# Second block: norms tile by tile, transpositions in four banks, first heads' loads ahead of the stores, reciprocals by pairs

## The chip, the cores and the metric

One core of one Trainium2 chip runs the whole program in one launch. The metric is the device time of that core in microseconds (us), the median of the runs; smaller is better.

## The reference, cut to what matters

The input is 512 tokens of width 1024 in fp32. A first transformer block (attention, neighbourhood attention, Fourier and convolution branches, a router with 16 experts) ends in `rms_norm(x, final_norm_g)`. The second block then runs two equal layers and a last norm:

```python
def rms_norm_2(x, w):
    y = xf * lax.rsqrt(jnp.mean(xf * xf, axis=-1, keepdims=True) + NORM_EPS)
    return (y * w).astype(x.dtype)

def hybrid_layer(x, ...):
    h = rms_norm_2(x, attn_norm_w)
    proj = h @ w_in
    mixed = concatenate([retention_mixer(...), dsa_mixer(...), dilated_mixer(...)])
    x = x + mixed @ w_out
    h = rms_norm_2(x, mlp_norm_w)
    return x + jnp.square(jax.nn.relu(h @ w_up)) @ w_down
```

Retention has 4 heads, the selecting attention (dsa) 4, the dilated attention 8, each 64 wide. The selecting attention scores each query against all earlier keys with 8 index heads and keeps the 128 best; the softmax runs over those.

## The kernel before, in words

Five engine programs are written out by hand and meet at semaphores. Tokens are 4 tiles of 128 rows (`X[:, i, :]`, 1024 wide), the inner dimension is 8 slices of 128 (`k`).

**Products.** A weight unit is 512 x 512. SP loads it (`unit`, L298), ACT rounds it to the short form (`hi`, L1269, into `WH`), DVE makes the remainder (`lo`, L1798, into `WL`), and PE runs three products for each of 4 slices and 4 output banks, 48 matmuls (`unit`, L715, line L736). A `blk` is two units on the same four banks. Weights lie in two slots that alternate.

**Norms of the second block.** There are five: one at the head of each layer, one ahead of each MLP, and the last. At the first block's end the tiles of the experts' output are combined on DVE (L2447 to L2453), then `final` (L2455) norms all four, and the layer's own norm follows. ACT squares and sums a tile of 1024 columns (`squares`, L1347), DVE turns four sums at once into reciprocal roots with 11 small instructions (`stats`, L1833, `rsqrt`, L1825) and scales the four tiles (`normed`, L1840). Then PE transposes (`turn_direct`, L760): 8 slices of 4 transpositions, in two banks of PSUM, so slice k waits until slice k-2 has been read. ACT rounds each slice (`split_direct`, L1337) and DVE makes its remainder (L1869). The first unit of products starts after all 32 transpositions.

**Index scores.** 24 steps (`index`, L1162 on PE, `relu`, L1659 on ACT, `index`, L2479 on DVE) stand between the output banks of the projections. In each, DVE adds a weighted score into `IX[tt]`; from step 8 on it also does one top-8 round for query tile 1 (`top_rounds`, L2496: a maximum and a replacement, 16 rounds for 128 keys). The rounds for tiles 2 and 3 stand among the six units of dilated projections, as `TOP_2` and `TOP_3` say (L113, L114). PE does the retention heads there too (`retention`, L1199).

**Attention.** `mixed_attention` (PE L933, ACT L1481, DVE L2078) takes 12 heads in 6 pairs. Per head: ACT rounds q and k (`rounded`), DVE makes remainders (`remainders`), PE scores four query tiles, DVE adds the bias and takes the extreme (`top`), ACT takes the exponential, PE transposes, ACT copies, PE multiplies with the values (`values`, L952) and then spreads the reciprocal sums of that head over 64 rows with four products against the identity (L963). DVE multiplies both (`put`). From pair 2 on PE does the output product in between, 3 matmuls per step (`product`), and the last 8 groups of 12 after the last pair (L1026). DVE adds them into X (`add`, L2113); ACT squares tile by tile as they are ready (semaphore `x5`).

**SP's order there.** Ahead of the first pair (`after_retention`, L440) SP waits until all stores of the layer are written, the one of the last projection among them, and until the retention heads have left the buffers; then it loads the bias, q, k and v of heads 4 and 5, and the two first blocks of `w_out` into `ST[0]` and `ST[1]`, which the stores have read. DVE releases PE and ACT for the attention with `sel_done` (L2601) after the last top-8 round.

The two layers are one loop of two turns on each engine.

```python
            def turn_direct(src, nk):
                for k in range(nk):
                    if k >= 2:
                        pe.wait_ge(sems["norm_lo"], T.at("norm_lo", k - 1))
                    for i in range(NT):
                        c0 = (k % 2) * 512 + i * P
                        mm = pe.transpose(TP[:, c0:c0 + P], src(i, k), IDN[:])
                    mm.then_inc(sems["norm_tr"], 1)
```

## Time and profile before

| | |
|---|---|
| median of 3 runs | 3216.89 us (3213.39 to 3218.46) |
| profiled execution, its own time | 3215.07 us |
| its span | 3213.0 us |
| PE busy (matmul) | 2753.3 us, 86% |
| DVE busy | 1742.8 us, 54% |
| ACT busy | 1271.9 us, 40% |
| ACT's rounding of a weight unit (L1275), mean of 131 | 1.91 us |
| DVE's remainder of one (L1803), mean of 131 | 2.29 us |
| loads of `w_up` units, median from issue to landing | 5.4 us |
| mean granted clock of TensorE | 0.934 |

The second block begins about 1580 us after the span's start; its two layers take about 800 us each. PE is busy for nearly all of the MLP parts; the stretches in which it is not lie around the norms, before the attention, and within it. A share of the granted clock of 1.00 is 2.4 GHz, 0.50 is 1.2 GHz.

### The profile page before, as it was taken

How to read it: one execution, taken by the hardware profiler on the slowest of the kernel's cores; microseconds unless marked ns; L12 is line 12 of the kernel's file. 1: busy time of each engine (PE TensorE's matmuls, PEld its weight loads, DVE VectorE, ACT ScalarE, POOL GpSimd, SP SyncE). 2: the span in 40 equal slices, each digit the busy share in tenths (PEclk: the TensorE clock that was granted, in tenths of full speed). 3: DMA queues.
4: the chain of work that ended last, by engine and by line, in shares of the span. 5: the costliest groups of instructions: out<-in, count | busy, mean ns of one | idle time of the engine just before them, and what ended most of it. 6: DMA issues, size and time to landing. Idle time of an engine off the chain costs nothing. (4 is left out here: it accounts for less than half of the span.)

```text
span 3213.0 us, 34356 instructions
## 1 busy us (share of the span) xinstructions
PE 2753.3 (86%) x11967; PEld 2064.3 (64%) x11967; DVE 1742.8 (54%) x2583; ACT 1271.9 (40%) x1739; POOL 114.6 (4%) x172
## 2 busy tenths in 40 slices
PE   3879989978798399999489969899999996989998
PEld 0167566556577277777376746688877573668886
DVE  1045146667575588888635755444443665544444
ACT  1033246656522177777433245222233314532222
POOL 2011000000000100000000100000000100000000
PEclk9989999989999699999779979899997997989999
DMA  8655343245253299999622442122222234222221
GB/s 316 217 159 151 114 109 91 81 103 129 90 180 118 111 354 371 386 371 366 232 61 82 118 109 85 62 95 91 91 87 63 92 99 129 65 66 92 95 100 72
DMA packets 241592, 466.35 MB, mean 145 GB/s; under 512 B 67864, under 2 KB 90640, under 8 KB 241455
## 3 DMA queue, kind: packets, MB, share of 16 engines
q1 hardware_dynamic: 226383, 413.73, 39.2%
q0 software_dynamic: 15072, 50.87, 4.7%
q8 instruction: 77, 1.26, 0.2%
q14 instruction: 60, 0.49, 0.1%
HBM read 399.83 MB, written 64.72 MB: 145 GB/s over the span
## 5 line engine op out<-in xcount | busy, mean ns | idle before, releaser
L1803 DVE TENSOR_TENSOR WL<-W,WH 128x2048 fp32r<-128x2048 f32 x131 | 300.2, 2292 | 502.2 <-ACT WH L1275 497.0
L1275 ACT ACTIVATE WH<-W 128x2048 fp32r<-128x2048 f32 x131 | 250.4, 1912 | 649.8 <-PE BKP L736 590.1
L736 PE MATMUL BKP<-hH,WH 128*128 128x512 f32 x896 | 357.4, 399 | 15.8 <-DVE hL L2201 13.2
L736 PE MATMUL BKP<-hL,WH 128*128 128x512 f32 x896 | 352.7, 394 | 0.0
L736 PE MATMUL BKP<-hH,WL 128*128 128x512 f32 x896 | 352.7, 394 | 0.0
L736 PE MATMUL BKP<-WH,aH 128*128 128x512 f32 (+1 forms) x544 | 215.3, 396 | 22.5 <-DVE aL L2396 10.4
L736 PE MATMUL BKP<-WL,aH 128*128 128x512 f32 (+1 forms) x544 | 211.4, 389 | 0.0
L736 PE MATMUL BKP<-WH,aL 128*128 128x512 f32 (+1 forms) x544 | 211.3, 388 | 0.0
L736 PEld LDWEIGHTS BKP<-hH,WH 128*128 128x128 f32 x896 | 171.4, 191 | 57.1 <-issue 20.3
L736 PE MATMUL BKP<-WH,hH 128*128 128x512 f32 (+3 forms) x512 | 201.2, 393 | 7.2 <-ACT Z L1326 3.1
L736 PE MATMUL BKP<-WH,hL 128*128 128x512 f32 (+3 forms) x512 | 194.2, 379 | 0.0
L736 PEld LDWEIGHTS BKP<-hL,WH 128*128 128x128 f32 x896 | 170.6, 190 | 36.6
L736 PEld LDWEIGHTS BKP<-hH,WL 128*128 128x128 f32 x896 | 171.4, 191 | 35.0
L736 PE MATMUL BKP<-WL,hH 128*128 128x512 f32 (+3 forms) x512 | 193.6, 378 | 0.0
L2290 DVE TENSOR_TENSOR X<-X,BKP 128x512 f32<-128x512 f32 x128 | 86.3, 684 | 144.6 <-PE BKP L736 144.6
L736 PEld LDWEIGHTS BKP<-WH,aH 128*128 128x128 f32 x544 | 103.3, 190 | 54.2 <-DVE aL L2396 21.4
L736 PEld LDWEIGHTS BKP<-WH,hH 128*128 128x128 f32 x512 | 104.5, 204 | 39.7 <-issue 24.7
L1125 PE MATMUL BKP<-WH,hH 128*128 128x512 f32 x276 | 113.9, 413 | 11.4 <-DVE WL L2416 8.1
L2416 DVE TENSOR_TENSOR WL<-W,WH 128x2048 fp32r<-128x2048 f32 x46 | 105.3, 2289 | 24.1 <-ACT WH L1614 23.8
L2416 DVE TENSOR_TENSOR WL<-G,WH 128x2048 fp32r<-128x2048 f32 x45 | 103.0, 2289 | 27.2 <-ACT WH L1614 27.2
L736 PEld LDWEIGHTS BKP<-WH,aL 128*128 128x128 f32 x544 | 103.3, 190 | 20.9
L736 PEld LDWEIGHTS BKP<-WL,aH 128*128 128x128 f32 x544 | 103.4, 190 | 19.6
(443 smaller groups left out, 5581.1 us busy)
## 6 DMA issues: line engine op xcount, KB each, us to landing
W<-in_w_expert_gu_dram SPq DMA_DIRECT2D x46, 1024.0 KB, 8.7
G<-in_w_expert_gu_dram SPq DMA_DIRECT2D x46, 1024.0 KB, 8.9
W<-in_w_in_dram SPq DMA_DIRECT2D x42, 1024.0 KB, 5.4
W<-in_w_up_dram SPq DMA_DIRECT2D x32, 1024.0 KB, 5.4
W<-in_w_down_dram SPq DMA_DIRECT2D x32, 1024.0 KB, 5.0
W<-in_w_expert_down_dram SPq DMA_DIRECT2D x24, 1024.0 KB, 8.0
G<-in_w_expert_down_dram SPq DMA_DIRECT2D x22, 1024.0 KB, 8.0
X<-in_w_in_dram SPq DMA_DIRECT2D x16, 1024.0 KB, 8.2
```

The source lines that it names most:

```text
L736: mm = pe.matmul(BK[j][:, 0:cols], lt, rh, start=start and a == 0, stop=stop and a == len(q) - 1, skip_group_check=True)
L1125: pe.matmul(dst, ah[:, k0 + kk, :], wh[:, kk, c], start=k0 + kk == 0, stop=False, skip_group_check=True)
L1275: act.activation(WH[s][:], W[s][:], ACT.Copy).then_inc(sems["w_hi"], 1)
L1803: v.tensor_tensor(WL[s][:], W[s][:], WH[s][:].bitcast(F32), ALU.subtract).then_inc(sems["w_lo"], 1)
L2290: v.tensor_tensor(xs, xs, BK[j], ALU.add).then_inc(sems[BANKS[j]], 1)
L2416: v.tensor_tensor(ring_l(m, s0), ring_w(m, s0), ring_h(m, s0).bitcast(F32), ALU.subtract).then_inc(sems["w_lo"], 1)
```

## The change

All of it is in the second block and the end of the first.

- **Norms by tile.** ACT squares half tiles of 512 columns as soon as they are summed (`half_square`, `tile_square`). DVE makes the root of one tile with 9 small instructions (`root`) and scales that tile (`tile_norm`). At the first block's end combining, the first block's norm and the layer's norm run interleaved over the tiles, and the first weight remainder (`lo`) stands ahead of them. In the attention's tail `tile_norm(j)` stands after the two additions of tile j, `lo` ahead of the first. In a layer's last MLP chunk it stands after the addition of tile j, and in the last layer the final scaling and the output do.
- **Transpositions.** Four banks (`TB`): 16 transpositions, then the first output bank of the first unit, then the other 16, then the rest (`normed_blk`).
- **Order of the loads.** SP waits for the stores after the values of heads 4 and 5 instead of before their q and k. ACT loads the table of the exponential and rounds q and k of head 4 within the copies of the last projection (`first_head`), DVE makes the remainders before `selected(3)`; `sel_done` is gone.
- **Top-8 rounds.** 8 rounds of tile 2 move into index steps 16 to 23; the others are spread one by one.
- **Reciprocals by pairs.** DVE writes the reciprocal sums out over 64 columns per head (two copies each), and PE spreads both heads with four products of 128 rows, once a pair.
- The loop over the two layers is written out, the weight slots swap from one to the other.

```diff
-TOP_2 = [2, 2, 1, 2, 1, 2, 2, 1, 2, 1]
-TOP_3 = [1] * 12 + [2] * 2
+TOP_2 = [1] * 8
+TOP_3 = [1] * 16
...
+        TINY = F[:, 1, 16:17]
+        RDW = [AT[:, c:c + 256].rearrange("p (t s c) -> p t s c", t=2, s=2) for c in (512, 1280)]
...
+        TB = [TP[:, 0:512], TP[:, 512:1024], SC[:, 0:512], SC[:, 512:1024]]
...
             def after_retention(s):
 
-                if s == 0:
-                    for b in range(3):
-                        sp.wait_ge(sems[f"st_written{b}"], T.next(f"st_written{b}", stored(STORES_2, b)))
-                        sp.sem_inc(sems["paused"], 1)
...
                 for s in range(2):
                     values(4 + s, s)
+                for b in range(3):
+                    sp.wait_ge(sems[f"st_written{b}"], T.next(f"st_written{b}", stored(STORES_2, b)))
+                    sp.sem_inc(sems["paused"], 1)
                 for u in range(2):
                     load(WOR[u], out_unit(wo, 0, u), ["side_landed0", "side_landed1", "side_back0", "side_back1"][u])
...
-                T.loop(2, layer)
+                for l in range(2):
+                    layer(l)
...
+            def normed_blk():
+
+                def turned(k):
                     for i in range(NT):
+                        mm = pe.transpose(TB[k % 4][:, i * P:(i + 1) * P], XN[:, i, k * P:(k + 1) * P], IDN[:])
                     mm.then_inc(sems["norm_tr"], 1)
+
+                def rest(j):
+                    if j == 0:
+                        for k in range(4, NK):
+                            turned(k)
+                pe.wait_ge(sems["norm_xn"], T.next("norm_xn", NT))
+                for k in range(4):
+                    turned(k)
+                unit(h, 0, "F", UN, True, False, ready="norm_lo", each=rest)
+                unit(h, 4, "F", UN, False, True, ready="norm_lo")
...
-                    pe.wait_ge(sems["head_rd"], T.next("head_rd"))
-                    for tt in range(NT):
-                        mm = pe.matmul(RD2[rows, tt * P:(tt + 1) * P], RDS[:, s, tt:tt + 1].to_broadcast([P, HD]), IDN[:], start=True, stop=True,
-                                       skip_group_check=True)
+                    if s == 1:
+                        pe.wait_ge(sems["head_rd"], T.next("head_rd", 2))
+                        for tt in range(NT):
+                            mm = pe.matmul(RD2[:, tt * P:(tt + 1) * P], RDW[tt // 2][:, tt % 2, :, :].rearrange("p s c -> p (s c)"), IDN[:],
+                                           start=True, stop=True, skip_group_check=True)
...
-                pe.wait_ge(sems["sel_done"], T.next("sel_done"))
-                mixed_attention()
-                pe.wait_ge(sems["norm_xn"], T.next("norm_xn", NT))
-                turn_direct(cols_of(XN), NK)
...
+            def half_square(i, hf, ready):
+                act.wait_ge(sems[ready], T.next(ready))
+                cols = slice(hf * UN, (hf + 1) * UN)
+                act.activation(XN[:, i, cols], X[:, i, cols], ACT.Square, scale=1.0 / 32,
+                               accum_out=SM[:, hf, i:i + 1]).then_inc(sems["norm_ss"], 1)
...
-            squares("norm", lambda i: X[:, i, :], NT, "x3")
-            act.wait_ge(sems["norm_rd"], T.next("norm_rd"))
+            hi()
+            tile_square(0, "x3")
+            for i in range(NT):
+                if i + 1 < NT:
+                    tile_square(i + 1, "x3")
+                tile_square(i, "x4")
...
+                def first_head(j):
+                    if j == 2:
+                        act.activation(TINY, IDN[:, 0:1], ACT.Exp)
+                        mixed_rounded(0, l)
+                gemm(copies(lambda j: ST[1][:, j, :], UN, 4, "st_filled1", first_head), None, False)
+                mixed_attention(l)
+                slot[0] ^= 1
                 hi()
+                for j in range(NT):
+                    for hf in range(2):
+                        half_square(j, hf, "x5")
...
+            def root(i, name, count):
+
+                v.wait_ge(sems[name + "_ss"], T.next(name + "_ss", count))
+                m, half, y, work = SM[:, 3, i:i + 1], SM[:, 3, 8 + i:9 + i], SM[:, 2, i:i + 1], SM[:, 3, 16 + i:17 + i]
+                link(v.tensor_scalar(m, SM[:, 0, i:i + 1], SM[:, 1, i:i + 1], EPS, ALU.add, ALU.add))
+                v.tensor_scalar(half, m, -0.5, None, ALU.mult)
+                link(v.tensor_scalar(y.bitcast(I32), m.bitcast(I32), -0.5, float(0x5F3759DF), ALU.mult, ALU.add))
+                for _ in range(3):
+                    link(v.scalar_tensor_tensor(work, y, half, y, ALU.mult, ALU.mult))
+                    link(v.scalar_tensor_tensor(y, work, 1.5, y, ALU.add, ALU.mult))
+                return y
+
+            def tile_norm(i, count):
+                y = root(i, "norm", count)
+                v.tensor_scalar(XN[:, i, :], X[:, i, :], y, None, ALU.mult).then_inc(sems["norm_xn"], 1)
...
-                    v.reciprocal(RDS[:, s, :], DENS[:, s, :]).then_inc(sems["head_rd"], 1)
+                    link(v.reciprocal(RDS[:, s, :], DENS[:, s, :]))
+                    for half in range(2):
+                        ins = v.tensor_copy(RDW[half][:, :, s, :],
+                                            RDS[:, s, 2 * half:2 * half + 2].unsqueeze(2).to_broadcast([P, 2, HD]))
+                    ins.then_inc(sems["head_rd"], 1)
...
-                    v.sem_inc(sems["x5"], 1)
+                        v.sem_inc(sems["x5"], 1)
+                    if j == 0:
+                        slot[0] ^= 1
+                        lo()
+                    tile_norm(j, 2)
...
+            lo()
...
+            combined(0)
+            for i in range(NT):
+                if i + 1 < NT:
+                    combined(i + 1)
+                finished(i)
+                if i:
+                    tile_norm(i - 1, 2)
+            tile_norm(NT - 1, 2)
...
                         if n >= 8:
                             top_rounds(1, 1)
+                        if n >= 16:
+                            top_rounds(2, 1)
...
-                        top_rounds(2, TOP_2[q]) if q < 10 else top_rounds(3, TOP_3[q - 10])
-                        if q == 9:
+                        top_rounds(2, TOP_2[q]) if q < 8 else top_rounds(3, TOP_3[q - 8])
+                        if q == 7:
                             selected(2)
...
+                mixed_remainders(0, l)
                 selected(3)
-                v.sem_inc(sems["sel_done"], 1)
...
+                def last_sum(hf):
+                    def go():
+                        for j in range(NT):
+                            out(j)
+                            xs = X[:, j, hf * UN:(hf + 1) * UN]
+                            v.tensor_tensor(xs, xs, BK[j], ALU.add).then_inc(sems[BANKS[j]], 1)
+                            v.wait_ge(sems[BANKS[j]], T.at(BANKS[j]))
+                            v.sem_inc(sems["x4"], 1)
+                            if hf == 1 and l == 0:
+                                tile_norm(j, 5 if j == 0 else 1)
+                            if hf == 1 and l == 1:
+                                y = root(j, "norm", 5 if j == 0 else 1)
+                                if j == 0:
+                                    v.wait_ge(sems["gf_landed"], T.next("gf_landed", 16))
+                                v.scalar_tensor_tensor(XN[:, j, :], X[:, j, :], y, GF, ALU.mult, ALU.mult).then_inc(
+                                    sems["out_ready"], 1)
+                    return go
```

## Rows read from the trace of the kernel before

**Rows 1.** Waits of PE over the span: engine, tile, line, releaser, us, times, longest
```profile
PE TPP L766 <- DVE BIG L1843: 84.6, 4, 49.5
```

**Rows 2.** Timeline of PE, first layer's head: start us, us, instruction [idle before <-releaser]
```profile
1617.43 1.97 PE L766 MATMUL TPP<-IDN,BIG 128*128 128x128 f32 x8 [49.48 <-DVE BIG L1843]
...
1627.09 0.78 PE L736 MATMUL BKP<-hH,WH 128*128 128x512 f32 x1
...
1649.77 0.20 PE L736 MATMUL BKP<-WH,hH 128*128 128x72 f32 x1
```

**Rows 3.** Windows: us, busy of PE, PEld, DVE, ACT, POOL, granted clock, DMA share, GB/s
```profile
1617.00:1627.00 10.00, 7.44 (x31) 5.83 (x32) 4.88 (x7) 4.50 (x7) 0.00 (x0) 0.50 0.00 1
...
2044.00:2048.00 4.00, 4.00 (x12) 3.23 (x12) 2.33 (x3) 2.97 (x3) 0.00 (x0) 0.50 0.02 4
```

**Rows 4.** Timeline of DVE, end of the first block, the same columns as rows 2
```profile
1581.39 0.75 DVE L2449 TENSOR_SCALAR BIG<-BIG,GATE 128x1024 f32<-128x1024 f32 x1 [20.84 <-DMA G<-y_scratch,SLOT]
...
1586.13 0.75 DVE L2449 TENSOR_SCALAR BIG<-BIG,GATE 128x1024 f32<-128x1024 f32 x1
...
1609.84 2.29 DVE L1803 TENSOR_TENSOR WL<-W,WH 128x2048 fp32r<-128x2048 f32 x1 [0.41 <-DVE X L2459]
```

**Rows 5.** Timeline of DVE between the layers: last addition, then first and twelfth instruction after
```profile
2403.24 0.69 DVE L2290 TENSOR_TENSOR X<-X,BKP 128x512 f32<-128x512 f32 x1 [2.03 <-PE BKP L736]
...
2409.63 0.17 DVE L1836 TENSOR_SCALAR SM<-SM 128x4 f32<-128x4 f32 x1
...
2411.92 2.74 DVE L1843 TENSOR_SCALAR BIG<-X,SM 128x1024 f32<-128x1024 f32 x4
```

**Rows 6.** Timeline of the end: ACT's last square, DVE's last three scalings
```profile
3200.81 1.06 ACT L1351 ACTIVATE BIG<-X 128x1024 f32<-128x1024 f32 x1 [1.57 <-DVEq L2294]
...
3205.74 4.15 DVE L2459 SCALAR_TENSOR_TENSOR BIG<-X,SM,AT 128x1024 f32<-128x1024 f32 x3 [0.16 <-DVE BIG L2459]
```

**Rows 7.** DMA issues, window 1569 to 1573: count, KB each, median us from issue to landing
```profile
W<-in_w_in_dram SPq DMA_DIRECT2D x2, 1024.0 KB, 11.0
```

**Rows 8.** Timeline of SP: the weight loads ahead of two norms
```profile
1570.25 1.20 SPq L305 DMA_DIRECT2D W<-in_w_in_dram  x2
...
1999.45 1.08 SPq L305 DMA_DIRECT2D W<-in_w_up_dram  x2
```

**Rows 9.** Timeline of PE, first layer's second norm
```profile
2034.61 1.97 PE L766 MATMUL TPP<-IDN,BIG 128*128 128x128 f32 x8 [11.81 <-DVE BIG L1843]
```

**Rows 10.** Timeline of DVE, ACT and PE at the end of the index steps
```profile
1773.00 0.56 DVE L2500 MAX8 TOP<-G 128x8 f32<-128x384 f32 x1
...
1774.47 0.56 DVE L2500 MAX8 TOP<-G 128x8 f32<-128x384 f32 x1
...
1764.00 0.60 ACT L1666 ACTIVATE F<-SCP 128x512 f32<-128x512 f32 x1 [1.82 <-DVE G L2488]
...
1766.05 1.97 PE L756 MATMUL TPP<-IDN,AT 128*128 128x128 f32 x8 [4.09 <-ACT ST L1326]
```

**Rows 11.** Timeline of SP, PE and DVE before the first layer's attention
```profile
1865.82 0.34 SPq L312 DMA_DIRECT2D ES<-in_k_dilbias_dram  x1
...
1873.69 0.48 PE L940 MATMUL SCP<-WH 128*128 128x128 f32 x1 [16.18 <-DVE WH L2083]
...
1857.77 0.68 DVE L2500 MAX8 TOP<-G 128x8 f32<-128x512 f32 x1
```

**Rows 12.** DMA issues, windows 1866 to 1868.6 and 1873.65 to 1876.8, columns as rows 7
```profile
KS<-kT_scratch SPq DMA_DIRECT2D x2, 128.0 KB, 3.1
...
KS<-kT_scratch SPq DMA_DIRECT2D x2, 128.0 KB, 7.8
```

**Rows 13.** Timeline of ACT, first pair of heads: rounding of the third head's q
```profile
1885.15 0.62 ACT L1485 ACTIVATE WH<-QS 128x512 fp32r<-128x512 f32 x1
```

**Rows 14.** Timeline of PE in the third pair of heads
```profile
1933.72 1.04 PE L963 MATMUL BKP<-IDN,F 128*64 128x128 f32 x8
1934.69 0.50 PE L940 MATMUL BKP<-WH 128*128 128x512 f32 x1
```

More of the change, by code:

```diff
@@ L700, in _ @@
             if not only_first:
-                T.loop(2, layer)
+                for l in range(2):
+                    layer(l)
             for s in range(2 if only_first else 3):
@@ L1259, in _ @@
             if not only_first:
-                T.loop(2, layer)
+                for l in range(2):
+                    layer(l)
         @block.scalar
@@ L1533, in mixed_attention @@
                 act.sem_inc(sems["head_ptc"], 2)
-                rounded(0)
                 exponential(0)
@@ L1740, in layer, with chunk @@
                 begin2("dv")
-                gemm(copies(lambda j: ST[1][:, j, :], UN, 4, "st_filled1"), None, False)
-                act.wait_ge(sems["sel_done"], T.next("sel_done"))
-                mixed_attention()
-                squares("norm", lambda i: X[:, i, :], NT, "x5")
-                act.wait_ge(sems["side_mm"], T.next("side_mm", 4 * NT))
-                hi()
-                act.wait_ge(sems["norm_rd"], T.next("norm_rd"))
-                split_direct(NK, hH[:], lambda k: AF[:, 3, k:k + 1])
-                def chunk(c, more=True):
+                def first_head(j):
[3 more added lines that the diff above has]
+                gemm(copies(lambda j: ST[1][:, j, :], UN, 4, "st_filled1", first_head), None, False)
+                mixed_attention(l)
+                slot[0] ^= 1
+                hi()
+                for j in range(NT):
+                    for hf in range(2):
+                        half_square(j, hf, "x5")
+                T.skip("side_mm", 4 * NT)
+                split_direct(NK, hH[:], lambda k: VT[:, V_MLP + l * 8 + k:V_MLP + l * 8 + k + 1])
+                def chunk(c, last=False):
                     def relu():
@@ L1761, in chunk @@
                     skip_banks()
-                    unit(None, more)
+                    if last:
+                        for j in range(NT):
+                            half_square(j, 0, "x4")
+                    unit(None, not last or l == 0)
                     skip_banks()
+                    if last:
+                        for j in range(NT):
+                            half_square(j, 1, "x4")
                 act.sem_inc(sems["paused"], 1)
                 T.loop(FF // UN - 1, chunk)
-                chunk(FF // UN - 1, False)
+                chunk(FF // UN - 1, True)
             def begin2(name):
@@ L1780, in _ @@
                     held[s] = 16 * [k for n, b, k in STORES_2 if b == s][-1]
-                T.loop(2, layer)
-                squares("norm", lambda i: X[:, i, :], NT, "x4")
+                for l in range(2):
+                    layer(l)
         @block.vector
@@ L2155, in mixed_attention @@
                 T.skip("head_o", 2)
-                remainders(0)
                 top(0, chosen)
@@ L2446, in _, with combined @@
             slot[0] = s0
-            for i in range(NT):
+            lo()
+            def combined(i):
                 v.wait_ge(sems[f"yc_landed{i}"], 32)
@@ L2618, in chunk @@
                     for hf in range(2):
-                        unit(add_x(hf, False, None if more or hf == 0 else "x4"), more or hf == 0)
+                        unit(last_sum(hf) if last else add_x(hf, False), not last or hf == 0 or l == 0)
                         skip_banks()
@@ L2622, in layer @@
                 T.loop(FF // UN - 1, chunk)
-                chunk(FF // UN - 1, False)
-            T.loop(2, layer)
-            final("norm", lambda i: XN[:, i, :], "out_ready", GF)
+                chunk(FF // UN - 1, True)
+            for l in range(2):
+                layer(l)
 def tables():
```

130 lines of the change are left out of this document (53 added, 77 removed).

## The prediction

> **What bounds the kernel now.** I began with the list of PE's waits, since PE is busy 86% of the span and only what it waits for can be taken away. The largest entry is the one on the scaled rows of a norm: 84.6 us in four waits, the longest 49.5 [rows 1]. The longest is at the first block's end and holds the gathers of the experts' output; the others are 11.8 us each. Then the timeline of the first norm: after the wait PE transposes from 1617.43 to 1627.09, 9.66 us for 32 transpositions, because two banks go round; the 96 products after them end at 1649.77, so 0.227 us each once the clock is up [rows 2]. In the ten microseconds of transpositions the granted clock is 0.50, that is 1.2 GHz, and it can stay there for four more microseconds of products [rows 3]. Ahead of the attention PE is idle for 16.18 us [rows 11]. At the end of the index steps it is idle for 4.09 us behind ACT, and ACT behind DVE [rows 10]. These are the places that the change touches, and in the rest PE is the bound.
>
> **The norms' chains on DVE.** Today 11 small instructions make four roots in 2.29 us [rows 5], 0.21 each. The new root has 9, one of them unlinked, but three take as their scalar what the instruction before or two before wrote. I take 2.0 us; bounds 1.7 (nine at 0.19) and 2.4 (nine at the old rate and three gaps of 0.16, as before the last scaling, [rows 6]). It is paid per tile.
>
> *End of the first block.* From the first combining to the first transposition are 36.0 us [rows 2, 4]. New: combining 4 x 4.74 = 19.0 [rows 4]; eight roots 16.0; four scalings with the gain 4 x 1.44 = 5.8 (4.15 for three with the gap, [rows 6]); four plain scalings 2.7 [rows 5]: 43.5. The remainder of the weights, 2.29 us [rows 4], leaves the chain but stands ahead of it: its load is issued at 1570.25 and takes 11.0 [rows 7, 8], so it lands at 1581.3, the rounding adds 1.9, the remainder ends at 1585.5, and combining starts 4.1 later than at 1581.39. Together 4.1 + 43.5 - 36.0 = **+11.6 us**. ACT's squares lie beside it.
>
> *Between the layers.* Additions follow each other every 2.72 us (0.69 and 2.03 of idle, [rows 5]). A tile now costs addition 0.69, half square with its signals 0.9 (half of 1.06, [rows 6], and reading the sum), root 2.0, scaling 0.69: 4.3, so DVE and not PE sets the pace. ACT squares the last half tile of the unit before first, then rounds, DVE makes the remainder: the chain begins near 2398.1 instead of 2395.1 and ends at 2415.3. Today the transpositions begin at 2414.7 (2.74 after 2411.92). **+0.6 us**.
>
> *After the attention, twice.* Here the groups of products take 2.72 each too, 5.44 per tile, and a tile costs DVE 1.4 + 0.9 + 2.7 = 5.0, so it nearly keeps pace. `lo` in front costs a start: load at 1999.45 [rows 8], 5.4 to land, rounded 2007, remainder done 2009.6, first tile 2012.3; the bank for the fifth group comes free at 2013.0, where PE wanted it at 2011.8: a wait of 1.3. The last group ends at 2024.0, its tile is scaled at 2028.3, against 2034.6 [rows 9]: **-6.3 us** each, -12.6.
>
> *The end.* Four tiles of 0.69 + 0.9 + 2.0 + 1.4 = 5.1 from the first addition, 8.2 before the last at 3200.0 [rows 6]: 3212.3 against 3209.9. **+2.4 us**.
>
> **Transpositions, four times.** Today 9.66 us stand ahead of the products. New: 16 transpositions, at the low clock 0.23 each, 3.65 us; products of the first bank wait for nothing that the low clock would not cost; 16 more take 1.85 us at the high clock, 3.65 at the low one. Saved 4.2 or 2.4. The transpositions did not bring the clock up, the products did [rows 3]; so I take nearly the low one: **-3.2 us** each, -12.8; bounds -4.2 and -0.4 (2.4 less the 2.0 that four further microseconds of products at 0.50, as in [rows 3], would lose, if the pause in the products keeps the clock down).
>
> The Trainium skill (TensorE: Matmul & The Clock Gate, Part 4: PE-mode transpose) says that the full clock does not engage for transpositions, which don't count as activity. By that the 16 in the midst of the first unit speak against this change: -0.4 instead of -3.2 each, and the sum would be some 11 us higher. The row of ten microseconds of transpositions at 0.50 agrees.
>
> **Top-8 rounds.** A round of 384 columns takes 1.47 us [rows 10]. Eight go into index steps 16 to 23. DVE has no idle time to speak of there: the last rectified score on ACT starts at 1764.00 as DVE's step 21 releases it, then ACT copies the transposed rows and PE goes on [rows 10]. Ahead of step 21 stand five of the new rounds: **+7.4 us** per layer, +14.8; four or six of them would be 5.9 or 8.8. What leaves the projections after it leaves PE's time untouched, PE being the bound there.
>
> **First heads' loads.** DVE has one round instead of two after 1857.77: 1859.4; two remainders of 0.7: PE begins at 1860.9 instead of 1873.69 [rows 11], -12.8. The load of the table falls into ACT's idle time. What is late next: the stores, still complete near 1865.8 [rows 11]; behind them SP issues 2 MB of `w_out`, and only then q and k of the third head, the last at 1869.5. Issued like that they took 7.8 us, not 3.1 [rows 12]: 1877.3. ACT needs them 12.8 before 1885.15 [rows 13], at 1872.4. Less traffic lies in front than today, so I take a stall of 4.0; bounds 0 and 5. **-8.8 us** per layer, -17.6.
>
> **Reciprocals.** Of two spreadings of 0.97 (1933.72 to 1934.69, [rows 14]) one is left: 6 x 0.97 = 5.8 per layer, on a PE that is the bound from the third pair on. DVE pays a link and two small copies per head, 0.55, mostly in idle time; I give back 1.0. **-9.5 us** in both; bounds -11.6 and -4.
>
> The written-out loop I cost at nothing: no row shows a wait at its turn; bounds -1 and +2.
>
> **Sum.** +11.6 +0.6 -12.6 +2.4 -12.8 +14.8 -17.6 -9.5 = -23.1. On the profiled execution's 3215.1 us that gives 3192.0; the median of the runs lies 1.8 above that execution: **3194 us**.
>
> **Rivals.** (1) *The rounds hide.* If DVE's line through the index steps had slack, the 14.8 fall away: 3179. For it: DVE has rounds enough elsewhere. Against: every rectification in that stretch names DVE. 0.13. (2) *The third head's loads come in time*, because the early heads' traffic is gone: 8.0 less, 3186. For it: 3.1 us for the same load without `w_out` ahead. Against: `w_out` still is ahead. 0.15. (3) *The start is not won*: QS of the second head, the stores or the released banks hold PE where it was: 17.6 more, 3211. That would be a change that doesn't do what it says; nothing in the rows shows such a hold. 0.06. (4) *Slower: the first unit of each norm runs at 1.2 GHz.* Its 48 products are broken by 16 transpositions after the twelfth; if the clock then comes up only after the unit, 38 products more than today cost 0.2 extra, with the transpositions 8.6 us per norm instead of the 0 in the sum: 34 more, 3228. It decides from 23.1 / 4 = 5.8 us per norm, 29 products. For it: four microseconds of products at 0.50 after the transpositions today. Against: elsewhere the products rose within 3 us. 0.07.
>
> The Trainium skill's rule named above is the one behind this rival; read in full, it gives 3228 as well.
>
> **Numbers.** The forecast has 0.59, with its own range 3186 to 3203 (roots -5 to +6 over some 18 of them on a path, transpositions -4 to +10, the rest +-4). The range of 8 in 10 takes in rival 2 and most of rival 1, and the upper bounds of transpositions and reciprocals: 3175 to 3209. A measurement of this kernel tells 0.2%, 6.4 us, from no change. Faster by more: 0.84, within: 0.07 (rival 3 and the upper end), slower: 0.09.
>
> **What would show it.** Right: transpositions at the first block's end begin near 1629, not 1617; the pairs between layers near the old distance; after the attention PE idle for 5 us instead of 11.8; PE's wait for the transposed rows at the index steps' end grows from 4.1 to 11.4; the wait ahead of the attention falls from 16.2 to 3.4; a new wait of ACT for KS in the first pair; L963's successor 96 times instead of 192. Wrong: no growth at the index steps, a chain of roots under 1.7 us, a clock of 0.50 through the first units, or a first pair of heads that takes over 6 us longer.

## The result, and the profile after

The changed kernel takes **3194.19 us** (median of 4 runs, 3189.33 to 3204.03), against 3215.78 for the kernel before in the same measurement: a ratio of 0.9937, 95% interval 0.9923 to 0.995. The forecast was 3194. The total is right; most of its terms are not, and this part is about them.

The page of the kernel after, beginning:

```profile
span 3202.2 us, 32605 instructions
## 1 busy us (share of the span) xinstructions
PE 2752.6 (86%) x11871; PEld 2061.8 (64%) x11871; DVE 1776.4 (55%) x2777; ACT 1272.3 (40%) x1786; POOL 117.8 (4%) x172
```

The waits of PE over the span (engine, tile, line, releaser, us, times, longest); the first line answers to [rows 1]:

```profile
PE TPP L769 <- DVE BIG L1913: 76.0, 4, 56.4
...
PE SCP L953 <- DVE WH L2123: 34.1, 14, 5.8
...
PE TPP L761 <- ACT ST L1337: 11.1, 4, 5.6
...
PE SCP L1180 <- ACT F L1685: 8.7, 4, 4.3
...
PE SCP L1221 <- DMA ES<-in_k_decay_dram: 7.4, 2, 4.1
```

The wait at the first block's end has grown from 49.5 to 56.4 and those of the other norms have shrunk. The last two lines are all but new: in the kernel before, PE waited 1.1 us in all for ACT at that place of the index steps, and never for the table of the first retention head, which no step of the forecast names.

**How to compare.** The profiled execution of the kernel after is its slowest of four. It ends the experts' last product at 1578.74, that of before at 1567.95, and the others of this study lie between 1568.5 and 1576.2, although no kernel changes anything ahead of it. So I compare from that product on: 1645.05 us were left before, 1623.46 after, **-21.6**. By stage, each from one event on PE to the next (the 72-column products are the first narrow ones of a layer's projections; the index steps begin behind them):

| stage | before | after | difference | forecast |
|---|---|---|---|---|
| last product to first transposition | 49.5 | 56.4 | +6.9 | +11.6 |
| to the 72-column products, layer 0 / 1 | 32.3 / 33.0 | 27.5 / 27.0 | -4.8 / -6.0 | -3.2 / -3.2 |
| to the first scores of the attention | 223.9 / 223.4 | 223.3 / 223.5 | -0.7 / +0.1 | -5.4 / -5.4 |
| to the transpositions of the second norm | 160.9 / 161.4 | 158.9 / 158.4 | -2.0 / -3.0 | -7.1 / -7.1 |
| MLP of layer 0, to layer 1's transpositions | 380.1 | 373.1 | -7.0 | -2.6 |
| MLP of layer 1 and the output | 380.5 | 375.4 | -5.1 | -0.8 |
| sum | | | -21.6 | -23.1 |

The forecast's column is the sum of its terms by stage (before the attention, for one, 7.4 less 12.8). The stages are off by 1.6 to 5.5 us each, and the errors cancel. One trace stands for each kernel here, and stretches that two kernels have in common can differ by 2 us.

PE's timeline at the first norm, against [rows 2, 3], and the windows there (us, busy of PE, PEld, DVE, ACT, POOL, granted clock, DMA share, GB/s):

```profile
1635.11 1.94 PE L769 MATMUL TPP<-IDN,BIG 128*128 128x128 f32 x8 [56.38 <-DVE BIG L1913]
1636.85 1.91 PE L769 MATMUL SCP<-IDN,BIG 128*128 128x128 f32 x8
1638.41 0.77 PE L741 MATMUL BKP<-hH,WH 128*128 128x512 f32 x1
...
1641.79 1.03 PE L769 MATMUL TPP<-IDN,BIG 128*128 128x128 f32 x8
1642.66 1.04 PE L769 MATMUL SCP<-IDN,BIG 128*128 128x128 f32 x8
```

```profile
1635.00:1639.00 4.00, 3.89 (x18) 3.82 (x19) 1.84 (x3) 2.27 (x4) 0.00 (x0) 0.50 0.54 142
1639.00:1641.00 2.00, 2.00 (x9) 1.66 (x8) 1.17 (x2) 0.48 (x1) 0.00 (x0) 0.85 0.41 102
1641.00:1643.00 2.00, 2.00 (x17) 1.79 (x16) 0.00 (x0) 0.58 (x1) 0.00 (x0) 1.00 0.00 0
```

The clock is up after the third product, and the second sixteen transpositions run at full speed. Next, SP's timeline at the end of the index steps of layer 0 (the 21.89 us hold the wait between the two weight loads), then DVE's and PE's. SP's second weight load goes out as DVE's remainder ends, at 1795.2, and the table behind it at 1797.84:

```profile
1773.71 21.89 SPq L308 DMA_DIRECT2D W<-in_w_in_dram  x2
...
1797.84 0.51 SPq L315 DMA_DIRECT2D ES<-in_k_decay_dram  x1
```

```profile
1792.91 2.29 DVE L1833 TENSOR_TENSOR WL<-W,WH 128x2048 fp32r<-128x2048 f32 x1
```

```profile
1784.01 1.97 PE L761 MATMUL TPP<-IDN,AT 128*128 128x128 f32 x8 [4.93 <-ACT ST L1337]
...
1806.13 2.68 PE L1221 MATMUL SCP<-QS,KS 64*128 64x512 f32 x4 [4.14 <-DMA ES<-in_k_decay_dram]
1808.73 0.80 PE L741 MATMUL BKP<-hH,WH 128*128 128x512 f32 x1
```

And SP, then PE and ACT around the attention's start, where [rows 11 to 13] were read. PE's waits are those ahead of the first, second, third and fifth head; ACT waits 5.75 us for the third head's k:

```profile
1885.57 1.62 SPq L315 DMA_DIRECT2D VS<-v_scratch  x2
1891.42 0.92 SPq L315 DMA_DIRECT2D ST<-in_w_out_dram  x2
1892.44 0.47 SPq L315 DMA_DIRECT2D QS<-qT_scratch  x1
```

```profile
1885.88 0.47 PE L953 MATMUL SCP<-WH 128*128 128x128 f32 x1 [3.32 <-DVE WH L2123]
...
1893.21 0.45 PE L953 MATMUL SCP<-WH 128*128 128x128 f32 x1 [3.60 <-DVE WH L2123]
...
1906.77 0.45 PE L953 MATMUL SCP<-WH 128*128 128x128 f32 x1 [5.75 <-DVE WH L2123]
...
1930.97 0.30 PE L953 MATMUL SCP<-WH 128*128 128x128 f32 x1 [2.67 <-DVE WH L2123]
```

```profile
1903.97 0.63 ACT L1502 ACTIVATE WH<-QS 128x512 fp32r<-128x512 f32 x1 [5.75 <-DMA KS<-kT_scratch]
```

### The profile page after: what moved, and what is told of

The parts are those of the page before. It is cut to its first block and busy times, and to the rows that moved or that the text cites. A ratio compares the mean times of both kernels' runs of the same rounds, so it can differ in the third digit from the quotient of the medians.

```text
span 3202.2 us, 32605 instructions
## 1 busy us (share of the span) xinstructions
PE 2752.6 (86%) x11871; PEld 2061.8 (64%) x11871; DVE 1776.4 (55%) x2777; ACT 1272.3 (40%) x1786; POOL 117.8 (4%) x172
## 5 line engine op out<-in xcount | busy, mean ns | idle before, releaser
L741 PE MATMUL BKP<-hH,WH 128*128 128x512 f32 x896 | 358.3, 400 | 16.2 <-DVE hL L2250 14.1
L2339 DVE TENSOR_TENSOR X<-X,BKP 128x512 f32<-128x512 f32 x112 | 75.6, 685 | 120.3 <-PE BKP L741 120.3
L741 PEld LDWEIGHTS BKP<-WH,aH 128*128 128x128 f32 x544 | 103.3, 190 | 54.2 <-DVE aL L2445 21.6
L741 PEld LDWEIGHTS BKP<-WH,hH 128*128 128x128 f32 x512 | 104.1, 203 | 39.7 <-issue 20.9
```

The costliest lines, as they stand in the source:

```text
L741: mm = pe.matmul(BK[j][:, 0:cols], lt, rh, start=start and a == 0, stop=stop and a == len(q) - 1, skip_group_check=True)
L2339: v.tensor_tensor(xs, xs, BK[j], ALU.add).then_inc(sems[BANKS[j]], 1)
```

## The experiments

Each edit is made to the kernel after unless said otherwise. "Aligned" is the time of the profiled execution from the experts' last product to the end, against 1623.46.

### The rounds out of the index steps

```diff
-TOP_2 = [1] * 8
-TOP_3 = [1] * 16
+TOP_2 = [2, 2, 1, 2, 1, 2, 2, 1, 2, 1]
+TOP_3 = [1] * 12 + [2] * 2
...
-                        if n >= 16:
-                            top_rounds(2, 1)
```

> The kernel after the change with its eight rounds of the third tile's top-8 search taken out of the index steps 16 to 23 again (spread over the projections as in the kernel before). Theory: the rounds cost twice, once because five of them stand ahead of the last rectification (5.1 us from the first 72-column product to the transpositions at the index steps' end), and once more because DVE comes out of the index steps late, frees the weight buffer late, and with it SP's queue, so that the table of the first retention head lands late (a PE wait of 4.14 us that the kernel before did not have) and the projections end some 3 us later still. Then each layer gives back 12, the wait for the table goes to 0, and the kernel takes about 3170. Rival A, the sum of my forecast: only the 5 to 7.4 us at the index steps come back per layer, the wait for the table stays near 4: about 3180 to 3184. Rival B: the rounds at the end of the projections hold the first head's remainders instead, the wait ahead of the attention grows from 3.3 to 8 or more, and the kernel takes 3180.

**3164.30 us** (3160.40 to 3169.61), aligned 1589.93: 33.5 less. From the 72-column products to the attention 12.9 us come back in layer 0 and 13.7 in layer 1; the rest lies mostly in the attention, where the third head's load came earlier (PE waits 3.04 and 5.24 us for it instead of 5.75 and 5.81). Both new waits of PE are gone, and ahead of the attention PE waits 5.06 instead of 3.32, so rival B is there, at 1.7 us. The theory stands, and the kernel is 6 us faster than it said: of the 12.9 and 13.7 us, the index steps up to the transpositions at their end show 7.7 and 9.0, the rest comes behind them.

### The table's loads ahead of the weights

```diff
-                blk(w2, 1992)
+                unit(w2[0:UN, bass.ds(1992, UN)])
                 retention_head(1, 1)
                 retention_head(0, 0)
+                unit(w2[UN:2 * UN, bass.ds(1992, UN)])
```

> The kernel after the change, rounds in the index steps as they are, with the loads of the first two retention heads (their tables among them) put in SP's queue ahead of the last weight load that they now follow. Theory: they are late only because that weight load waits in SP's queue for a buffer that DVE, busy with the new rounds, frees late; put ahead of it, PE's wait of 4.1 us for the table goes to 0 in both layers, and since these 4 us are on PE's path the projections end 4 us earlier: 3186. If the weight load itself is what is late, PE waits for its remainder instead and nothing is won: 3194.

**3181.81 us** (3180.25 to 3185.51), aligned 16.2 less. PE no longer waits for the table. But the stretch from the index steps' end to the attention gets 7.2 and 6.5 us shorter (101.87 to 94.69, 102.39 to 95.90), not 4 as expected. The windows after the wait in the kernel after, and at the same place in this one, show the rest:

```profile
1804.00:1808.00 4.00, 1.87 (x4) 0.81 (x4) 0.44 (x1) 0.00 (x0) 0.00 (x0) 0.86 0.97 305
1808.00:1812.00 4.00, 4.00 (x10) 2.59 (x9) 1.90 (x5) 0.00 (x0) 0.00 (x0) 0.50 0.03 11
1812.00:1816.00 4.00, 4.00 (x15) 2.88 (x14) 1.09 (x3) 0.60 (x1) 0.00 (x0) 0.79 0.00 0
```

```profile
1796.00:1800.00 4.00, 4.00 (x16) 2.65 (x15) 2.98 (x6) 0.19 (x1) 0.00 (x0) 1.00 0.59 182
1800.00:1804.00 4.00, 4.00 (x22) 3.31 (x21) 1.84 (x6) 0.78 (x2) 0.00 (x0) 1.00 0.29 113
```

By the three granted clocks 0.86, 0.50 and 0.79 over 4 us each, the clock is at half for some 6.8 us after the wait of 4.14, which loses 3.4: 7.5 together, an estimate from these windows, against the 7.2 measured. So this wait costs about 7, and only because the loads stood behind a weight load in SP's queue.

### The w_out loads behind the third and fourth head's

```diff
-                for b in range(3):
+                for b in (2,):
                     sp.wait_ge(sems[f"st_written{b}"], ...)
                     sp.sem_inc(sems["paused"], 1)
-                for u in range(2):
-                    load(WOR[u], ...)
...
                 def later(i):
                     ... # q and k of two heads
+                    if i == 0:
+                        # waits for st_written0 and 1, then both loads of WOR
```

> The kernel after the change with SP's wait for the stores of the dilated q and v, and the two w_out loads behind it, moved behind the q and k loads of the third and fourth head (the wait for the store of k stays in front). Theory: the third head's loads are late because they stand in SP's queue behind that wait (issued 6.6 us after the attention's start instead of at it) and behind 2 MB: PE's waits for the third and fourth head (5.75 and 2.67 us) go back to some 1.9 and 0.4, 5 to 6 us per layer, and the kernel takes 3183 to 3185. Rival: the loads are slow because eight of them run beside each other, whatever stands ahead: the waits keep over two thirds of their length, 3191 or more; or w_out then comes too late for its rounding in the second pair, and a wait of that size appears there: 3194.

**3187.11 us** (3182.74 to 3190.31), aligned 1613.23: 10.2 less. SP issues the third head's loads 2.5 and 2.0 us after the attention's start instead of 6.6 and 6.5, and each lands 3.5 to 4.7 us after its issue instead of 7.7 to 9.6. PE waits 2.91 and 1.63 us for the third and the fifth head in layer 0 (5.75 and 2.67 in the kernel after, where the expectation takes the fifth for the fourth) and 2.62 and 1.38 in layer 1. In this kernel ACT rounds the third head's q without a wait, and SP's order and ACT's row are

```profile
1882.92 1.13 SPq L315 DMA_DIRECT2D QS<-qT_scratch  x1
...
1892.83 0.61 ACT L1506 ACTIVATE WH<-QS 128x512 fp32r<-128x512 f32 x1
```

So the place in the queue was the cause of the late load. What is left of PE's wait, half of it and more than the 1.9 expected, is no longer the load: DVE makes this remainder only at 1896.42, between its steps for the retention heads' norm. No wait for `w_out` appears.

### The first heads' loads behind the stores again

```diff
             def after_retention(s):
+                if s == 0:
+                    # the waits for st_written0 to 2, taken out of mixed_heads
...
-                        mixed_rounded(0, l)          # ACT, among the last projection
+                mixed_rounded(0, l)                  # at the attention's start
...
-                mixed_remainders(0, l)               # DVE, before selected(3)
+                mixed_remainders(0, l)               # before top(0, chosen)
```

> The kernel after the change with the first heads' loads behind the stores again, and ACT's and DVE's split of the first head back at the attention's start. Theory: the wait ahead of the attention goes from 3.3 back to some 16 us, but the third and fourth head's loads then are in time again (their waits fall from 5.75 and 2.67 us to 1.9 and 0.4), so of the 12.9 us per layer some 5 to 6 are given back and the kernel is 14 to 16 us slower, 3209. Rival: the stall of the third head has nothing to do with the early start; then the kernel is 26 us slower, 3220.

**3214.51 us** (3204.45 to 3221.07, 10 runs), 20 more, aligned 18.5 more. The stretch up to the attention is 12.35 and 12.72 us longer, the attention 3.79 and 3.44 shorter: 8.6 and 9.3 net per layer. The forecast had 8.8, out of 12.8 and a stall of 4.0. The kernel is slower than the 14 to 16 us that this run's expectation gave: the waits for the third and the fifth head fall only to 3.52 and 2.28.

### The reciprocals head by head

```diff
-                    if s == 1:
-                        pe.wait_ge(sems["head_rd"], T.next("head_rd", 2))
-                        # four spreadings of both heads, 128 columns of weights
+                    pe.wait_ge(sems["head_rd"], T.next("head_rd"))
+                    # four spreadings of this head, 64 columns of weights
...
-                    link(v.reciprocal(RDS[:, s, :], DENS[:, s, :]))
-                    for half in range(2):
-                        ins = v.tensor_copy(RDW[half][:, :, s, :], ...)
+                    v.reciprocal(RDS[:, s, :], DENS[:, s, :]).then_inc(sems["head_rd"], 1)
```

> The kernel after the change with the reciprocals spread head by head again, as in the kernel before (one copy less pair of DVE copies and link per head, twelve spreadings of four on PE instead of six per layer). Theory: each spreading left out took 0.97 us of PE; where PE is the bound that is worth its time, so the kernel gets 8 to 11.6 us slower, about 3203 to 3206, all of it between the attention's start and the second norm of each layer. Rival: the attention's pairs are bound by the chain from scores over DVE and ACT back to PE, the spreadings lie in PE's idle time, and the difference is under 3 us: 3197 or less.

**3194.46 us** (3188.56 to 3196.24): no difference, as the rival said. The aligned time is 5.6 less, but in this execution the third head's load landed 1.5 to 2 us earlier, and the stretch before the attention of layer 0 was 1.8 shorter. So the edit was tried once more on a kernel in which the loads are in time, below.

### The norms of the first block's end for four tiles at once

```diff
-            combined(0)
-            for i in range(NT):
-                if i + 1 < NT:
-                    combined(i + 1)
-                finished(i)
-                if i:
-                    tile_norm(i - 1, 2)
-            tile_norm(NT - 1, 2)
+            for i in range(NT):
+                combined(i)
+            lo()
+            roots("norm", 2 * NT)        # one root for four tiles
+            # four scalings with the gain, a root, four plain scalings
```

> The kernel after the change with the two norms at the first block's end done for four tiles at once, as in the kernel before: four combinings, then one root for four tiles, four scalings, one root, four scalings; the weights' remainder stands between the last combining and the root. Theory: 16 small instructions per tile and chain cost 8 roots of 1.84 us, two roots of four tiles cost 4.6, so that the first transposition begins some 6 us earlier after the last product of the experts (57 to 58 us instead of 63.7), and the kernel takes 3188. Rival: ACT's squares of four tiles then stand on the chain and the gain is under 2: 3192 or more.

**3185.94 us** (3182.06 to 3188.59), aligned 13.0 less. The first transposition comes 48.98 us after the last product instead of 56.37, so 7.4 less, and even before the 49.48 of the kernel before:

```profile
1625.18 1.94 PE L769 MATMUL TPP<-IDN,BIG 128*128 128x128 f32 x8 [48.98 <-DVE BIG L2519]
```

The other 5.6 lie in the attention and in the index steps of layer 0, where this edit changes nothing. In the index steps it is the clock: 0.77 on the mean of the 30 us behind the 72-column products, 0.72 in the kernel after. For the attention no cause was looked for.

### All transpositions ahead of the products

```diff
                 for k in range(4):
+                for k in range(NK):
+                    if k >= 4:
+                        pe.wait_ge(sems["norm_lo"], T.at("norm_lo", k - 3))
                     turned(k)
-                unit(h, 0, "F", UN, True, False, ready="norm_lo", each=rest)
+                unit(h, 0, "F", UN, True, False, ready="norm_lo")
```

> The kernel after the change with all 32 transpositions of a norm ahead of the products, still in four banks, none among the first unit's products. By the remainders' pace no bank holds PE, so PE works without a gap. Theory: what kept the clock at 0.50 in the kernel before was the idle gaps of 0.71 us after each eight transpositions, and transpositions without gaps bring the clock up about 4.2 us after the first like any other work: the clock rises before the last transposition, from the first transposition to the first 72-column product are 27.5 to 28.5 us as now, and the kernel takes 3194. Rival (transpositions do not count as work): the clock is 0.50 through all 7.3 us of them and for some 4 us of products: 31 us or more, 3.7 more per norm, 3209.

**3196.04 us** (3194.17 to 3196.37). From the first transposition to the 72-column products are 28.16 and 28.11 us, 0.7 and 1.1 more than after and far from 31. PE's timeline and the windows at the first norm of this kernel:

```profile
1629.60 1.94 PE L769 MATMUL TPP<-IDN,BIG 128*128 128x128 f32 x8 [56.59 <-DVE BIG L1915]
1631.34 1.91 PE L769 MATMUL SCP<-IDN,BIG 128*128 128x128 f32 x8
1633.05 1.91 PE L769 MATMUL TPP<-IDN,BIG 128*128 128x128 f32 x8
1634.75 1.39 PE L769 MATMUL SCP<-IDN,BIG 128*128 128x128 f32 x8
1635.90 0.48 PE L741 MATMUL BKP<-hH,WH 128*128 128x512 f32 x1
```

```profile
1629.00:1635.00 6.00, 5.40 (x26) 5.43 (x27) 3.60 (x6) 3.44 (x6) 0.00 (x0) 0.50 0.42 100
1635.00:1636.00 1.00, 1.00 (x9) 1.00 (x8) 0.90 (x2) 0.94 (x2) 0.00 (x0) 0.77 0.67 171
1636.00:1638.00 2.00, 2.00 (x11) 1.67 (x10) 1.97 (x4) 2.00 (x3) 0.00 (x0) 1.00 0.00 0
```

The clock rises while the last eight transpositions run (1.39 us instead of 1.91), and the first product already takes 0.48 instead of 0.77. No product had run since the wait of 56.59 us. The theory stands. Placing half of the transpositions among the first unit's products, as the kernel after does, is worth about a microsecond per norm at most, and the aligned time, 1621.49, is no longer than after.

### The kernel before with four banks

```diff
-                    if k >= 2:
-                        pe.wait_ge(sems["norm_lo"], T.at("norm_lo", k - 1))
+                    if k >= 4:
+                        pe.wait_ge(sems["norm_lo"], T.at("norm_lo", k - 3))
...
-                        mm = pe.transpose(TP[:, c0:c0 + P], src(i, k), IDN[:])
+                        mm = pe.transpose(TB[k % 4][:, i * P:(i + 1) * P], src(i, k), IDN[:])
```

> The kernel before with nothing but four banks instead of two for the 32 transpositions of each norm of the second block, all of them ahead of the products. Theory: the whole gain at the transpositions (24 us over four norms: 4.8, 6.6, 6.0 and 6.6 from the first transposition to the 72-column products or the first addition) comes from the banks, since two banks make PE idle 0.7 us after each eight transpositions and that keeps the clock at 0.50 through them and into the products: 3192. Rival: banks alone leave PE waiting for ACT's and DVE's splits, as the split of eight row groups takes 6.4 us in any case, and the gain is the 2.4 us per norm of my forecast or less: 3206.

**3198.11 us** (3191.47 to 3200.52), 18.8 less than the kernel before, between theory and rival. The four stages with a norm's transpositions are 4.5, 6.0, 5.2 and 4.8 us shorter, 20.5 together where the theory had 24; aligned it is 23.9 less than before. PE's second eight transpositions in the kernel before, and its last eight and first product in this one:

```profile
1620.11 1.97 PE L766 MATMUL TPP<-IDN,BIG 128*128 128x128 f32 x8 [0.71 <-DVE hL L1876]
```

```profile
1627.58 1.04 PE L766 MATMUL SCP<-IDN,BIG 128*128 128x128 f32 x8
1628.38 0.47 PE L737 MATMUL BKP<-hH,WH 128*128 128x512 f32 x1
```

The three stops of 0.71 us are gone, and the last eight already run at the full clock (1.04 us for eight, 1.97 before). This one part alone is worth nearly as much as the whole change.

### The kernel before with its loop over the layers written out

```diff
-            T.loop(2, layer)
+            for l in range(2):
+                layer(l)
```

> The kernel before with nothing but the loop over the two layers written out on every engine. Theory: the turn of the loop hides behind the norm's wait, and the time is that of the kernel before, 3213 to 3217, also by stage. Rival: the longer program is fetched in another way; the profiled executions of the changed kernels reach the last product of the experts at 1573 to 1579 us, that of the kernel before at 1568, and if the written-out loop does this, it shows here as well, with 5 us or more in the first block and 3220.

**3210.03 us** (3204.04 to 3216.11, 10 runs), a ratio of 0.998 (0.9969 to 0.9991) to the kernel before, aligned 6.3 less. The largest part, 4.4, is in the stage that holds the loop's turn. DVE's timeline there, of the kernel before and of this one:

```profile
2403.24 0.69 DVE L2290 TENSOR_TENSOR X<-X,BKP 128x512 f32<-128x512 f32 x1 [2.03 <-PE BKP L736]
2407.13 2.29 DVE L1803 TENSOR_TENSOR WL<-W,WH 128x2048 fp32r<-128x2048 f32 x1 [3.21 <-issue]
```

```profile
2402.95 0.69 DVE L2294 TENSOR_TENSOR X<-X,BKP 128x512 f32<-128x512 f32 x1 [2.03 <-PE BKP L738]
2403.78 2.29 DVE L1807 TENSOR_TENSOR WL<-W,WH 128x2048 fp32r<-128x2048 f32 x1
```

DVE stood idle for 3.21 us at the turn, ahead of the remainder that the norm's chain follows. So the turn does not hide, against the theory, and the first block is not slower (its last product ends at 1569.32), against the rival. With the four banks that is 18.8 and 6.7 us by the medians, more together than the 21.6 of the whole change; if the two add, which no run tests, the rest of the change nets nothing, its gains and losses cancel.

### Three at once

The kernel after with the rounds out of the index steps, the `w_out` loads moved, and the norms of the first block's end for four tiles, by the edits above.

> The kernel after the change with three of the experiments at once: the rounds out of the index steps, the w_out loads behind the third and fourth head's q and k, and the norms of the first block's end for four tiles at once. Theory: the three act at different places, so the terms add: from 3164 of the first of them 7 for the norms and 5 to 10 for the loads, 3147 to 3152. Rival: with the rounds back DVE is the bound in the first pairs of heads, and the loads bring nothing more: 3157.

**3154.07 us** (3150.91 to 3155.70), a ratio of 0.9802 (0.9786 to 0.9819) to the kernel before; aligned 1582.29. The rounds alone gave 3164.30; 10 more came, a little less than the 12 to 17 expected of the other two.

### Three at once, the reciprocals head by head

The same with the reciprocals' edit above.

> The combination of three experiments (3154) with the reciprocals spread head by head again. Theory: in the pairs of heads where PE sets the pace a pair takes 16.5 us with one spreading and 17.3 with two, in the first two pairs, where waits for loads and for the chain over DVE set it, nothing is won: four pairs by 0.85, 3.4 us per layer, 6 to 7 slower in all, 3160. Rival: the gain of the steady pairs is given back by DVE's copies and their link, and the time is 3154 within 2.

**3156.96 us** (3154.41 to 3159.01), aligned 1581.23, so 2.9 more by the medians and 1.1 less by the traces. Pairs four and five of the heads take 17.4 and 17.3 us in layer 0 against 16.5 and 16.5: the 0.9 per pair is there. It is given back earlier: PE's waits for the remainders of the third to fifth head are 1.56, 0.49 and 1.93 here and 2.21, 1.94 and 2.60 with the reciprocals by pairs, 2.8 us together (1.4 in layer 1). What is left is at most some 3 us of the whole kernel.

### Three at once, with the other two norms for four tiles

```diff
                             v.sem_inc(sems["x4"], 1)
-                            # root and scaling of tile j
+                        if hf == 1:
+                            roots("norm", 2 * NT)
+                            # four scalings
```

> The combination of three experiments (3154) with the norm between the layers and the last norm also done for four tiles at once, after the last addition; the norms after the attention stay tile by tile. Theory: where PE delivers a half tile every 2.72 us and a tile costs DVE 4.3, tile by tile ends 2.7 us later between the layers and some 1.5 later at the end than four tiles at once: 3150. Rival: ACT's half squares after the last addition put their 1 us on the chain and nothing is won: 3154.

**3151.33 us** (3143.47 to 3152.08), a ratio of 0.979 (0.9774 to 0.9806): the fastest. Aligned 4.8 less than three at once: 4.3 in the stage that ends between the layers (373.63 to 369.37), 1.3 after PE's last product (13.27 to 11.95). The rival, that nothing is won, did not come.

## Why the prediction was right, and where it was not

That the total came out is luck. Three terms were too hopeful, by 23.5 us together (after the attention, the rounds, the reciprocals); the others left out or undersized gains of 18.1, and 3.9 more is in no term.

- **End of the first block**, +11.6: it was +6.9. The chain was right, 42.3 us from the first combining to the transpositions against 43.5; a root took 1.84 us instead of the 2.0 taken. The start was wrong: I took the median of two loads, 11.0, for the landing of the first. It landed 7.9 after its issue, and combining began 0.6 later than before, counted from the last product, not 4.1.
- **Between the layers**, +0.6: from the last unit's steady additions to the transpositions it was -0.4, as a sum of two errors. The loop's turn gave 3.1 (in the kernel before with its loop written out, by the same events), which I had cost at nothing with the words that no row shows a wait there. A row did, and I had not shown it. Against a written-out loop, tile by tile costs 2.7 here; four tiles at once gave back 4.3.
- **After the attention**, -6.3 each: -4.7 each, from 31.82 to 27.11 us between the first product of the tail and the transpositions. PE's wait is 4.32 instead of 11.81, as forecast 5, but the tail's products take some of it.
- **The end**, +2.4: +0.3 after the last product. A tile took 4.58 us, not 5.1.
- **Transpositions**, -12.8: -22.8 (4.8, 6.6, 6.0 and 5.3, taken to the 72-column products, in the MLPs to the first addition in layer 0 and to PE's last product in layer 1). Here the mechanism was wrong and not only the size. I held that products and not transpositions bring the clock up, and took the sixteen at the low one. In the kernel before, the clock stayed at 0.50 while PE stopped for 0.71 us after each eight transpositions; with four banks and nothing else changed there are no stops, and it rose during the last eight. Products are not always quicker at it: in the trace with all transpositions ahead, those of the experts that began at 1564.39 took 0.63 us each until 1570.5, and then 0.40. Stops and low clock were one loss, and the outer bound of 4.2 each, which counts only a part of it, was too tight.
- **Top-8 rounds**, +14.8: +26.6, the term that is off by most. The 7.4 at the index steps is nearly right: 7.7 and 9.0 between the kernels with and without the rounds. PE's wait there was to grow from 4.1 to 11.4; it is 4.93, with a new one of 4.29 ahead of it. Missed was what else DVE releases: the weight buffer, on which SP's queue waited with the retention heads' loads behind it. I had named what leaves the projections, not what is queued behind SP.
- **First heads' loads**, -17.6: -17.9, and by the mechanism given: the wait fell from 16.18 to 3.32, and the stores' wait with 2 MB behind it held the third head. ACT's wait for its k is there, and the first pair takes 20.9 and 20.4 us instead of 16.7, close to the stall of 4.0.
- **Reciprocals**, -9.5: about -1, between 0 and -3. The 0.97 per pair is there as 0.9 in pairs four and five. In the first pairs DVE is on the path, and I had given its extra copies back at 1.0 per layer where 2.8 and 1.4 are waited for. The bound of -4 was still too good.
- **The loop**, 0: -3.1 at the turn (above), of 6.3 that the written-out loop gives aligned.

With 6.9, -0.4, -9.4, +0.3, -22.8, +26.6, -17.9 and -1 the sum is -17.7 of the -21.6 (the loop is in the second term). The rest, and a microsecond more, is a gain of 2.6 per layer between the 72-column products and the index steps' end of the kernel without the rounds against the kernel before (113.73 against 116.28 us in layer 0). 1.7 of it is there after the first 30 us, and it is the clock: on the mean of these 30 us it was 0.66 in the kernel before and 0.72 in the kernel without the rounds in layer 0, and 0.72 and 0.77 in layer 1. The other kernels with four banks, some with the same code there, show 0.72 or 0.77 in either layer, so a part of it can be scatter. The written-out loop shows 0.9 of the whole. What makes the remainder was not tried.

Of the rivals, hidden rounds did not happen (26.6 instead of 0), and neither did a start that is not won (the wait fell to 3.32). The third head's loads in time did not happen either, but can be had by an edit. The slower case, a first unit at 1.2 GHz, was the opposite of what happened: the clock is up after the third product. The Trainium skill (TensorE: Matmul & The Clock Gate, Part 4: PE-mode transpose) states that the full clock does not engage for transpositions. The trace of the kernel before agreed only in appearance: with all 32 ahead and no stops, the clock rose from 0.50 during the last eight. The measurement decides: for the fp32 transpositions of 128 x 128 in this kernel that rule does not hold.

## What to carry to other kernels

When work is moved onto an engine, follow each thing that the engine releases, through the other queues: eight small rounds on DVE held a weight buffer, that held SP, and SP held a small table that PE waited for. A wait of four microseconds on PE cost nearer seven here, since the clock had to come up again; and short regular stops, as two banks made them, kept it down all along. A sum that comes out right proves none of its terms: compare stage by stage, and search the trace for idle time put down to "issue" before an edit is costed at nothing.

## What was not expected of the hardware

Transpositions without gaps brought the granted clock from 0.50 to 1.00 as products do: with no product before them, it was 0.50 from 1629 to 1635, 0.77 in the next microsecond and 1.00 behind it. The turn of the outer loop left DVE idle for 3.21 us. And with 2 MB ahead in the queue, eight loads of 128 KB took 7.5 to 9.6 us each: the third head's four, issued from 1892.44 to 1894.34, were there at 1903.95, while without `w_out` ahead the third head's took 3.5 to 4.7.
